# Two heads' recurrence scores in one row, and two groups of stick-breaking value products in one row

## The reference, cut to what matters

```
b = cumsum(log f)
scores[t, s] = sum_d q[t, d] * k[s, d] * exp(b[t, d] - b[s, d])     (s <= t)
o = scores @ v + (q * exp(b)) @ state
```

```
z = q k^T / 8
a[t, s] = sigmoid(z[t, s]) * prod over s < j < t of (1 - sigmoid(z[t, j]))     (s < t)
o = rmsnorm(a @ v)
```

## Time and profile before

| what | value |
|---|---|
| median of three runs | 3735.88 us (3731.62 to 3745.44) |
| the profiled execution, its own time | 3732.92 us |
| its span | 3731.2 us |
| TensorE busy | 3659.1 us, 98% |
| VectorE busy | 2041.5 us, 55% |
| ScalarE busy | 1499.7 us, 40% |
| GpSimd busy | 700.7 us, 19% |
| granted TensorE clock, mean | 0.996 |

### The profile page before, as it was taken

One profiled execution on the slowest core, in us unless ns is written; L12 is line 12 of the kernel. 1 busy time (PEld: TensorE's weight loads), 2 busy tenths in 40 slices (PEclk: granted clock), 3 DMA queues, 4 the chain that ended last, 5 costly groups with the idle time before them and its releaser, 6 DMA issues.

```text
span 3731.2 us, 62641 instructions
## 1 busy us (share of the span) xinstructions
PE 3659.1 (98%) x25576; PEld 3125.7 (84%) x25576; DVE 2041.5 (55%) x3773; ACT 1499.7 (40%) x2727; POOL 700.7 (19%) x405
## 2 busy tenths in 40 slices
PE   8999999999999999998999999999999999999999
PEld 6888788978897887976888778888777899998998
DVE  5658624541645355457655665555554365545555
ACT  4332431231232354566566564545553332223222
POOL 2001130000000000233233340100000154414442
PEclk9999999999999999999999999999999999999999
DMA  8756687557665877866676666555433666666664
GB/s 307 279 185 236 222 287 259 193 212 237 217 216 180 287 251 240 268 230 208 211 241 212 200 220 220 184 168 162 137 117 148 237 237 235 236 235 226 237 237 181
DMA packets 215534, 820.57 MB, mean 220 GB/s; under 512 B 22096, under 2 KB 71504, under 8 KB 152144
## 3 DMA queue, kind: packets, MB, share of 16 engines
q1 hardware_dynamic: 215248, 816.57, 62.6%
HBM read 615.15 MB, written 201.33 MB: 219 GB/s over the span
## 4 chain that ended last, share of the span: by engine, by line
PE 90%; DVE 5%; ACT 2%; issue 1%; DMA 1%; SPq 0%; POOL 0%; DVEq 0%; ACTq 0%; POOLq 0%
PE bank L1550 86%; PE bank L1554 4%; DVE P L2757 1%; DVE P L2759 1%; DVE SH L2451 0%; DVE R L2372 0%; SPq L3003 0%; DVE Z1a L2419 0%; ACT P L2158 0%; ACT P L2157 0%; DVE Tb L2509 0%; DMA slot<-Wd 0%; DMA R<-X1d 0%; ACT L2157 0%; ACT Z1a L1992 0%
## 5 line engine op out<-in xcount | busy, mean ns | idle before, releaser
L1550 PE MATMUL bank<-slot,Z0b 128*128 128x512 f32 (+1 forms) x3504 | 708.8, 353 | 6.3 <-DVE AF L2441 4.5
L1550 PEld LDWEIGHTS bank<-slot,Z0b 128*128 128x128 f32 x3504 | 561.4, 189 | 97.1 <-DVE AF L2441 5.2
L1550 PE MATMUL bank<-Z1a,slot 128*128 128x512 f32 (+1 forms) x2568 | 610.5, 381 | 9.4 <-DVE slot L2307 9.4
L1550 PE MATMUL bank<-Z1b,slot 128*128 128x512 f32 (+1 forms) x2568 | 606.8, 380 | 6.0 <-DVE Z1b L2419 5.9
L1550 PEld LDWEIGHTS bank<-Z1a,slot 128*128 128x128 f32 x2568 | 446.9, 190 | 98.7 <-DVE slot L2307 9.4
L1550 PEld LDWEIGHTS bank<-Z1b,slot 128*128 128x128 f32 x2568 | 444.9, 189 | 96.5 <-DVE Z1b L2419 7.2
L2959 POOL TENSOR_TENSOR slot<-raw,slot 128x1024 fp32r<-128x1024 f32 x110 | 290.2, 2646 | 645.4 <-ACT slot L2041 645.3
L2372 DVE SCALAR_TENSOR_TENSOR R<-bank,small,R 128x512 f32<-128x512 f32 x352 | 260.7, 748 | 185.6 <-PE bank L1550 185.1
L2725 DVE TENSOR_SCALAR_CACHE_REDUCE P<-bank 128x512 f32<-128x512 f32 (+3 forms) x320 | 189.2, 608 | 199.3 <-PE bank L1550 198.7
L1550 PE MATMUL bank<-KS,DQ 128*128 128x512 f32 (+3 forms) x960 | 281.5, 389 | 8.8 <-DMA KS<-Kd 4.4
L2975 POOL TENSOR_TENSOR Z0b<-AF,Z0b 128x512 fp32r<-128x512 f32 x88 | 132.9, 1510 | 803.7 <-ACT Z0b L2231 803.7
(11 more groups left out here) (260 smaller groups left out, 5511.7 us busy)
## 6 DMA issues: line engine op xcount, KB each, us to landing
slot<-Wd SPq DMA_DIRECT2D x350, 1024.0 KB, 5.4
Wd<-slot SPq DMA_DIRECT2D x130, 1024.0 KB, 7.3
raw<-in_wts_dram SPq DMA_DIRECT2D x210, 512.0 KB, 4.5
DQ<-Qd SPq DMA_DIRECT2D x192, 128.0 KB, 3.8
slot<-Wd SPq DMA_DIRECT2D x40, 512.0 KB, 6.2
DV<-Vd SPq DMA_DIRECT2D x60, 256.0 KB, 4.5
KS<-Kd SPq DMA_DIRECT2D x24, 512.0 KB, 7.8
KS<-Kd SPq DMA_DIRECT2D x24, 384.0 KB, 7.4
```

Source lines behind the costliest of these rows:

```text
L1550: return e.matmul(o, a, b, start=start, stop=stop, skip_group_check=True)
```

## The change

In the recurrence lane both heads' scores of a level are put together, with one `yield` before them, at the later of the two heads' ready times; their planned cost is 400 ns each. In the attention's back lane the stick-breaking heads (e = 4, 5) collect two groups before their value products are put, both without a `yield` between; the differential heads (e < 4) go on as before with one. No instruction is added or left out, and no operand changes; the order in which the planner writes the engines' streams does.

```diff
--- before.py
+++ after.py
@@ -488,16 +488,14 @@
         t = [0.0, 0.0]
         for j in range(2):
             t[j] = P.put(("hg k", u, j), ("dve", 1400))
-        for j in range(2):
-            yield t[j]
-            t[j] = P.put(("hg sc", u, 0, j), ("pe", 800)) + 200
         for i, L in enumerate((0,) + LEVELS):
+            x = max(t)
+            yield x
+            for j in range(2):
+                t[j] = P.put(("hg sc", u, i, j), ("pe", 400), after=x) + 200
             for j in range(2):
                 yield t[j]
                 t[j] = P.put(("hg l", u, i, j), ("dve", 2200 if L == 16 else 1350 if L <= 16 else 1050), after=t[j])
-                if L < 64:
-                    yield t[j]
-                    t[j] = P.put(("hg sc", u, i + 1, j), ("pe", 800 if 2 * L <= 16 else 500), after=t[j]) + 200
         yield ("ev", ("A", s, 2 * hp, 1))
         for j in range(2):
             yield t[j]
@@ -721,7 +719,7 @@
             n = SUB * s + 128 * (qt + 1)
             nb = n // 128
             last = qt == NT - 1 and (half == 1 or e < 4)
-            pend = None
+            pend = []
             for g in range(0, nb, 4):
                 m = len(self.tp_uses)
                 if m > 1:
@@ -730,10 +728,15 @@
                 w = min(4, nb - g)
                 self.tp_uses.append(("tr", u, g // 4))
                 t = P.put(("tr", u, g // 4), ("pe", 107 * w), ("act", 200 + 108 * w), after=P.end[("cb", u)])
-                if pend:
-                    yield from self.av(u, i, *pend, last)
-                pend = (g // 4, w, t)
-            yield from self.av(u, i, *pend, last)
+                if e < 4 and pend:
+                    yield from self.av(u, i, pend, last)
+                    pend = []
+                pend.append((g // 4, w, t))
+                if len(pend) == 2:
+                    yield from self.av(u, i, pend, last)
+                    pend = []
+            if pend:
+                yield from self.av(u, i, pend, last)
             if e < 4:
                 P.put(("o", u), ("act", 540), after=P.clock["pe"] + 200)
             else:
@@ -741,12 +744,14 @@
             if last:
                 P.add(self.finish_diff(i, s, e) if e < 4 else self.finish_stick(i, s, e), slack=SLACK_C)
 
-    def av(self, u, i, g, w, t, last):
-        yield t
+    def av(self, u, i, groups, last):
+
+        yield max(max(t, self.P.end["ld", i, "v", g]) for g, w, t in groups)
         s, e = self.heads[i]
-        self.P.put(("av", u, g), ("pe", (215 if e < 4 else 110) * w), after=max(t, self.P.end[("ld", i, "v", g)]))
-        if last:
-            self.get(i + 1, ("v", g))
+        for g, w, t in groups:
+            self.P.put(("av", u, g), ("pe", (215 if e < 4 else 110) * w), after=max(t, self.P.end[("ld", i, "v", g)]))
+            if last:
+                self.get(i + 1, ("v", g))
 
     def finish_diff(self, i, s, e):
         P = self.P
```

## The result

| | before | after |
|---|---|---|
| median | 3733.75 us (4 runs: the three above and 3728.69) | 3698.74 us (3696.74 to 3700.56, 4 runs) |
| profiled execution, own time | 3732.92 us | 3697.3 us |
| span | 3731.2 us | 3695.6 us |
| TensorE busy | 3659.1 us | 3629.3 us |
| score rows / stick-breaking rows | 116 / 147 | 64 / 96 |

The ratio is 0.9902, with a 95% interval from 0.9877 to 0.9926; 3707 us was predicted. The page after, TensorE's line and the chain by engine, answers to the earlier trace rows: as full as before, and nearly as much of the chain.

A forecast was written before the change was run, and what follows sets the result against it. TensorE, busy 98% of the span, was taken to bound the kernel. Merges save 15.1 + 13.5 = 28.6 us, waits zero: 3732.9 becomes 3704.3, plus 3.0 to the median gives 3707 us; range 3691 to 3731.

The forecast's parts named there:

- What bounds the kernel: Whole kernel: TensorE busy 3659.1 of 3731.2 us, so nearly every nanosecond taken off it comes off the time.
- The price of a row: TensorE's runs of one matmul kind: merging two score rows saves 0.29 us, two stick-breaking rows 0.30 us.
- the alternating pattern: Stick-breaking value products alternating with transposes: two products and two transpose groups cost 2.26 us, merged 2.00, saving 0.26.
- The number of merges: Recurrence scores go from 116 rows to 64, 52 merges; stick-breaking from 147 to 96, 51 merges.
- The sum: Recurrence 15.1 us plus stick-breaking 13.5 us gives 28.6 us saved.
- the six merges in the loose stretch: Stick-breaking sub-block 1, stretch 1650 to 1800 us: TensorE idles there anyway, so these merges count zero.
- What moves: nothing: Recurrence units end some 7 us later, attention lane pauses fall from four to two; no cost to the time.
- The waits of the new order: zero, 13 us either way: TensorE's waits, some 52 us without the start: no net change, a quarter of them as bound.
- Rival 1: New order returns 10 to 28 us as new waits: 3717 to 3735 us, middle 3726; chance 0.18.
- Rival 2: Cost goes with the number of matmuls, not rows, so merging is worth nothing: 3736 us; chance 0.05.
- Rival 3: Recurrence: paired row stalls TensorE until the second head's copies end, losing 48 us: 3755 us; chance 0.07.
- The marks: Timeline signs: last recurrence scores (1186.6 us) 7 to 15 us earlier, last stick-breaking product (2852.2) 25 to 29 earlier.

## Why the prediction was right, point by point

- **What bounds the kernel.** Right for the whole change: 28 us of TensorE's work gone, none of it came back as waits, and the time fell by 35. It is not enough by itself: in each part alone the work went and the time stayed.
- **The price of a row.** Right. Rows of 64 records cost 0.89 us as read off, 61 rows more cost 0.30 each where 0.29 was taken, and over all kernels a row costs 0.31. In the alternating pattern 1.97 was measured for 2.00.
- **The number of merges.** Right: 64 and 96 rows, 52 and 51 merges.
- **The sum.** 28.6 us predicted, 27.9 of work measured. The parts are less exact than their sum: scores 12.7 (16.6 beside the load wait) for 15.1, values 15.2 (15.0) for 13.5. For the values the six merges in the loose stretch should not have been set to zero in the work; without that my figure was 15.3.
- **What moves: nothing.** Wrong for the edit in `av`. The prediction spoke of the lane's pauses and not of the value load that `av` now waits for. This edit was costed at nothing by leaving it out, and it was worth 16 to 18 us in the change: without it the time is 3716.50. That the kernel before needed no such wait hid it: TensorE idled 3.0 us before value products there, and 20 to 28 in each of the four other orders that lacked it. Without the edit the time would still have lain in the range, 9.5 us above the 3707 forecast; that the rest of the sum came out whole is owed to the edit, which was not reasoned: luck.
- **The waits of the new order: zero, 13 us either way.** The 21 waits add up to 63.0 us and not to 61, and the range was built with 10 and 11 us in place of the 13; neither changes the forecast. The size held for the change (7.6 us less, which is why the time fell by 35 us and not by 28) and the bound did not hold for orders in general: over the twelve other orders waiting went from 62.5 to 100.8 us against 70.1, and even with the load wait and slacks as before from 62.5 to 83.0, the heads set apart left out. The bound "a quarter of today's waits" had no ground; the kernel before sits near the low end.
- **Rival 1** (waits give part of it back) did not happen, but is what happened to each part alone, each of which lost more in waits and half clock (18.3 and 16.2 us) than it gained in work (12.7 and 15.2). **Rival 2** is refuted by the work of every merged kernel. **Rival 3** did not happen with the slack of 1500 ns; at 1000 ns it begins.
- **The marks.** The last recurrence scores came at 1178.9 us for 1186.6, 7.7 earlier, as said. The last stick-breaking product did not come 25 us earlier but 17 later, at 2869.2. That mark was wrong: the end of the program moved by 36 us and this product did not move with it. I take the attention's place against the main sequence to be free; no run tests that.

What stays open is which of the order's small waits (`Z1b` up, `P` down) make up the 7.6 us; I have no run that moves one of them alone.

## What to carry to other kernels

Where TensorE is full, look for short runs of matmuls on a part of its columns between full-width ones, read the cost of a run from start to start, and put runs of one shape side by side; count the runs, not the matmuls. When a schedule written ahead is changed, split the time into work and waiting before you judge it: a 15 us gain in work vanished in the waits of a new order here, and one instruction placed before its load had landed cost 11 us by itself. An edit that does nothing in today's order may be what keeps tomorrow's safe.

## What the runs showed of the hardware

An entry into and an exit from a column-tiled shape cost together about 0.3 us with 32 columns (a single row of 0.59 against 0.30 for 32 further records in the same row) and 0.34 to 0.40 with 64 (a single row of 0.78 to 0.80, two together 1.20 to 1.22). A part of the exit is behind the row, where the first full-width matmul takes 338 ns to the next start instead of 234. Between full-width shapes no such cost can be told from nothing: 31 rows fewer were worth at most 2.5 us. Narrow records in a row of four 32-column tiles start 8.5 ns apart on average (32 records in 0.26 us). The Trainium skill, "TensorEngine Tiling (Array Packing)", Tiling Modes, says that a change of mode drains TensorE; the runs here agree in that rows cost where the mode changes and not where it stays, and show the price, not the drain itself.

A value load of 256 KB landed after 4.5 us in the median of the kernel before and after 14.1 to 14.9 us at one place in the four orders that let TensorE wait for it; the loads issued around it took 9 to 16 us there too.
